# Delta rule: the next head's projection tiles dealt out in 11 portions of two to six per head instead of 18 of one to six

## What is computed

```
proj = rms_norm(x) @ w_in                       # q, k, v, z of each head
q, k, v = silu(conv(q)), silu(conv(k)), silu(conv(v))
q, k = l2_norm(q) * 128**-0.5, l2_norm(k)
m = strictly_lower(k_beta @ k.T * decay)
t_inv = inverse(eye + m)                        # triangular, unit diagonal
u, w  = t_inv @ v_beta, t_inv @ (k_beta * exp(g))
attn  = lower(q @ k.T * decay)
for each chunk:                                 # sequential
    v_new = u - w @ state
    o     = (q * exp(g)) @ state + attn @ v_new
    state = state * exp(g_last) + k_dec.T @ v_new
o = rms_norm(o) * silu(z)
```

## Time and profile before

| | before |
|---|---|
| median of 3 runs | 1638.53 us (1637.02 to 1641.39) |
| the profiled execution, its own time | 1640.73 us |
| its span in the profile | 1638.9 us |
| TensorE matmul busy | 1558.5 us, 95% of the span |
| VectorE busy | 624.2 us, 38% |
| ScalarE busy | 586.6 us, 36% |
| GpSimd busy | 577.8 us, 35% |
| mean granted TensorE clock | 0.986 of full speed |

### The profile page before, as it was taken

The page is one execution under the profiler, slowest core; times in us unless marked ns, Lnnn a source line. Parts: engine busy times, 40 slices in busy tenths (PEclk is TensorE's granted clock), DMA queues, the critical chain, the costliest instruction groups (busy, mean ns, idle before and its releaser), DMA issues.

```text
span 1638.9 us, 21277 instructions
## 1 busy us (share of the span) xinstructions
PE 1558.5 (95%) x7900; PEld 1277.1 (78%) x7900; DVE 624.2 (38%) x1014; ACT 586.6 (36%) x956; POOL 577.8 (35%) x286
## 2 busy tenths in 40 slices
PE   6899999999998989999999999887889999999998
PEld 6868878888787668888888887666668888888887
DVE  3336555665555432222122224677532222012210
ACT  6642243223332433322222234454533322222321
POOL 5531332223220234544434444211124443544442
PEclk9999999999999999999999999999999999999999
DMA  7411110111010123332333233111113332333222
GB/s 252 127 56 39 52 33 32 51 38 51 26 33 0 39 77 96 104 102 82 112 102 101 74 89 122 42 39 30 30 49 108 95 101 79 114 103 102 80 79 86
DMA packets 39208, 124.24 MB, mean 76 GB/s; under 512 B 4192, under 2 KB 5472, under 8 KB 39136
## 3 DMA queue, kind: packets, MB, share of 16 engines
q1 hardware_dynamic: 38976, 123.00, 25.0%
q10 hardware_dynamic: 160, 0.26, 0.1%
HBM read 120.89 MB, written 2.10 MB: 75 GB/s over the span
## 4 chain that ended last, share of the span: by engine, by line
PE 85%; DVE 6%; ACT 5%; issue 3%; DMA 0%; POOL 0%; SPq 0%; DVEq 0%; ACTq 0%
PE bank L548 66%; ACT ws L1044 4%; PE bank L713 3%; PE bank L711 2%; PE bank L699 2%; DVE ws L1426 1%; PE bank L977 1%; DVE ws L1432 1%; DVE act_lo L1432 1%; PE bank L847 1%; PE bank L810 1%; DVE ws L1435 1%; DVE ws L1429 1%; PE bank L736 1%; PE bank L1002 1%
## 5 line engine op out<-in xcount | busy, mean ns | idle before, releaser
L480 POOL TENSOR_TENSOR w_lo<-w_raw,w_hi 128x1024 fp32r<-128x1024 f32 (+1 forms) x250 | 537.8, 2168 | 949.8 <-ACT w_hi L1044 949.5
L548 PE MATMUL bank<-act_hi,w_hi 128*128 128x512 f32 (+1 forms) x1776 | 704.3, 397 | 10.0 <-POOL w_lo L480 4.4
L548 PE MATMUL bank<-act_hi,w_lo 128*128 128x512 f32 (+1 forms) x1776 | 681.0, 383 | 0.0
L548 PE MATMUL bank<-act_lo,w_hi 128*128 128x512 f32 (+1 forms) x1776 | 680.6, 383 | 0.0
L548 PEld LDWEIGHTS bank<-act_hi,w_hi 128*128 128x128 f32 x1776 | 336.2, 189 | 76.9 <-issue 7.8
L548 PEld LDWEIGHTS bank<-act_hi,w_lo 128*128 128x128 f32 x1776 | 335.6, 189 | 65.7
L548 PEld LDWEIGHTS bank<-act_lo,w_hi 128*128 128x128 f32 x1776 | 336.4, 189 | 63.8 <-issue 5.0
L1044 ACT ACTIVATE w_hi<-w_raw 128x1024 fp32r<-128x1024 f32 (+1 forms) x250 | 230.4, 953 | 89.1 <-PE bank L548 86.6
L1426 DVE TENSOR_TENSOR ws<-bank,ws 128x512 f32<-128x512 f32 x126 | 86.9, 690 | 371.5 <-PE bank L548 320.9
L1044 ACT ACTIVATE ws<-ws 128x512 f32<-128x512 f32 (+3 forms) x143 | 94.3, 670 | 189.2 <-DVE ws L1426 122.0
L1673 DVE TENSOR_TENSOR xT<-xT,bank 128x512 f32<-128x512 f32 (+1 forms) x48 | 33.0, 688 | 271.6 <-PE bank L548 271.6
(11 more groups left out here) (145 smaller groups left out, 1211.8 us busy)
## 6 DMA issues: line engine op xcount, KB each, us to landing
w_raw<-w_stream SPq DMA_DIRECT2D x154, 512.0 KB, 3.5
w_raw<-w_out SPq DMA_DIRECT2D x32, 384.0 KB, 3.2
w_raw<-w_down SPq DMA_DIRECT2D x32, 384.0 KB, 3.1
w_raw<-w_down SPq DMA_DIRECT2D x32, 320.0 KB, 3.2
ws<-x_in SPq DMA_DIRECT2D x1, 2048.0 KB, 8.4
ws<-mem_in SPq DMA_DIRECT2D x2, 512.0 KB, 4.0
out<-ws SPq DMA_DIRECT2D x1, 1024.0 KB, 4.2
sq_c<-squares_in SPq DMA_DIRECT2D x1, 768.0 KB, 6.3
```

The costliest lines, as they stand in the source:

```text
L480: nc.gpsimd.tensor_tensor(w_lo[:, s, 0:width * P], w_raw[:, s, 0:width * P], w_hi[:, s, 0:width * P].bitcast(F32), ALU.subtract).then_inc( ...
L548: mm = nc.tensor.matmul(acc, wt[:, c % RING, wsl], at[:, act0(k0 + k), off:off + n], start=(start and k == 0 and m == 0), stop=(stop and k ...
```

## The change

The same 32 tiles per head are issued, in the same order, by the same matmuls. The change moves where eleven of the portions stand in TensorE's list: projection 2 goes out as four portions of two tiles, each between P and TZ of levels 1 to 4, and no tile stands between TZ and the next P or in level 5. Projection 3 goes out as two tiles in each of the chunks 0 and 1 and four after the loop; nothing stands ahead of L723 or in chunks 2 and 3. The lists of the other engines are untouched.

```diff
-            LEVEL_FILL = (0, 2, 4, 6, 7, 8)
+            LEVEL_FILL = (0, 2, 4, 6, 8)
...
-                    if k <= 5:
-                        fill(2, range(LEVEL_FILL[k - 1], LEVEL_FILL[k - 1] + 1))
+                    if k <= 4:
+                        fill(2, range(LEVEL_FILL[k - 1], LEVEL_FILL[k]))
                     for g in range(2):
                         pe.wait_ge(S.p_done, n + g + 1)
...
                         mm.then_inc(S.tz_mm, 1)
-                    if k <= 3:
-                        fill(2, range(LEVEL_FILL[k - 1] + 1, LEVEL_FILL[k]))
-                fill(3, range(0, 1))
 
                 pe.wait_ge(S.tz_done, 12 * h + 12)
...
-                    fill(3, range(t + 1, t + 2))
+                    if t < 2:
+                        fill(3, range(2 * t, 2 * t + 2))
                     pe.wait_ge(S.v_done, n + 1)
...
                 mm.then_inc(S.o_done, 1)
-                fill(3, range(5, 8))
+                fill(3, range(4, 8))
```

## The result

The changed kernel takes 1662.8 us (median of 4 runs, 1661.4 to 1663.3) against 1640.0 us (median of 4, 1637.0 to 1642.3). The ratio is 1.0136, with a 95% interval of 1.0122 to 1.0149: 20 to 24 us slower. The forecast was 1658.5 with a range of 1654 to 1663. The span of the profiled execution grew from 1638.9 to 1661.5 us, by 22.6. One count ahead needs setting right: the change doesn't move eleven portions. Projections 2 and 3 went out in 14 portions per head and now go out in 7; with the four portions of projections 0 and 1, which stand as before, that makes the 18 and the 11 of the title.

A forecast was written before the change was run, and what follows sets the result against it. TensorE's matmul work, plus its holes, was taken to bound the kernel. Levels +1.80 and the part behind them +1.05 made +2.85 per head, +20.0 us over seven heads: 1658.5 us, range 1654 to 1663.

The forecast's parts named there:

- The levels: Levels 1 to 5 of each head: 21.40 us against 19.60 now, +1.80 for the same eight tiles.
- the price of an open passage: TZ to the next P with no tile between: 0.56 us, from level 5 at 3.98 against level 4 at 3.42.
- The cover over the tap: In levels with two tiles between P and TZ, these hide DVE's convolution tap and multiplications with 0.66 us to spare.
- The passage from P to TZ costs nothing uncovered: Inside a level, no added time without tiles, since DVE multiplies the first half while P works on the second.
- Behind level 6: From level 6's first step through the chunk loop to the sum on L753: +1.05 us per head.
- chunk 0 to 1: Chunk loop, one tile more: from 2.11 to 2.80 us, +0.69.
- The sum: Levels and the part behind them: +2.85 us per head, +20.0 us for seven heads; head 7 unchanged.
- Printed idle only: Rival: only the idle that the profile prints is lost, 0.9 us per head, 6 us in all, 1645; 4%.
- Tap in the path: Rival: the two tiles don't hide DVE's tap and multiplications in three levels, +14 us, 1672; 4%.
- Falling clock inside the heads: Rival: one slow stretch per head at 0.53 of the clock, +12 us on top, 1670; 2%.
- Boundaries: Rival: boundaries between portions cost more than waits, so faster, 1634 with every wait hidden; over 0.41 us each needed; 2%.
- The idle that I named before the first state product: Sign: no idle before L746 of chunk 0, new idles before L746 of chunk 2 and L748 of chunk 3.

The follow-up runs named there:

- r2: Only projection 2's portions moved (pairs between first and second step of levels 1 to 4), projection 3 as in the kernel before: 1655.0 us against 1638.4, ratio 1.0096.
- r4: Against the kernel before, projection 2 in pairs behind the second step of levels 1 to 4, projection 3 as before: ratio 1.0049, heads 7.3 to 7.7 us longer.
- r6: Against the kernel before, same tiles with six more portion boundaries per head where TensorE isn't waited for: ratio 1.0007, heads 1.0 to 1.3 us longer.

## Why the prediction was right

**The levels.** Forecast 4.11, three of 4.67, 3.28, sum 21.40; measured 4.10, then 4.66, 4.67 and 4.66, then 3.28, and 21.37 from 304.92 to 326.29. The step that mattered was to read the price of an open passage from the lengths of levels 4 and 5 and not from the idle column, which prints 0.18 for what costs 0.60 (r2 against the rival's 4 us). That the printed idle falls short of the cost is what these rows show; it doesn't follow from the ends being computed.

**The cover over the tap.** The forecast left 0.66 to spare. In the profile after, tap and multiplications end at 311.18 and L711 starts at 311.85, 0.67 later, with no idle. Right.

**From one step to the next inside a level.** "The passage from P to TZ costs nothing uncovered" held in bare levels (3.28, as in the earlier trace rows) and was my reason for giving level 5 no cost, which was right. As a general statement it is wrong: r4 shows 0.33 for it when the level's own start is covered. VectorE needs some 0.6 from the end of L699's first half to the end of its multiplication, in r4 as below; the second half of L699 lasts only 0.44. In a bare level that second half comes late anyway and the multiplication hides behind its wait (in level 5 after, the first multiplication runs from 323.77 to 324.19, while L699's second half starts only at 323.90), so only one of the two passages is paid.

```profile
302.62 0.87 DVE L1424 TENSOR_TENSOR ws<-bank,sq_c 128x256 f32<-128x256 f32 x2 [0.48 <-PE bank L699]
```

That is VectorE in r4's level 2, whose L699 starts at 301.98: the first multiplication can't start before 302.62, and the second step follows at 303.10 where TensorE was through with L699 at 302.87.

**Behind level 6.** From L699 of level 6 to L720 it takes 3.56, 3.57 before: the tile gave back 0.01, for a forecast of 0.02. Up to the first state product it takes 2.61 (forecast 2.59), in the bare chunks 1.81 and 1.91 (forecast 1.82 and 1.86), and behind the loop 3.07 (forecast 3.09). One term was mis-sized: chunk 0 to 1 took 2.69 and not 2.80. I had added a tile to 2.11, but the 2.11 held the starting lag of a wait that the change removes: L746 to L748 of chunk 0 took 0.33 before (318.67 to 319.00) and takes 0.22 after (L744 to L746, 332.46 to 332.68), so 0.1 had to come off. The part from L720 to L751 is 12.09 against 11.11 before, +0.98 for a forecast of +1.07.

**The sum.** Forecast +2.85 per head, 20.0 in all. Measured 19.4 to 19.9 over the seven heads in three profiles of each kernel.

**The time.** 1658.5 forecast, 1662.8 measured, 4.3 more. Of these, 1.4 are the kernel before itself, whose median with a fourth run is 1640.0 and not the 1638.5 that I added to. The other 2.9 stand over the forecast difference of 20.0. The heads gave nothing to them; 3.1 us came from the start of the kernel in this pair. The range had 1.5 us for scatter of any kind, so it held the result with nothing to spare, and that it did is partly luck. The mechanism and its size are what the prediction had right.

**The rivals.** Printed idle only: refuted by r2, 12.1 to 12.4 against 4. I had also priced it too low: the printed idle of the seven heads rose by 7.9 us (from 7.6 to 15.5) and not by 6. Tap in the path: no idle before L711. Falling clock inside the heads: 1.00 over the seven heads in every profile, and no projection tile in them shows the longer durations of a slow stretch. The Trainium skill ("TensorE: Matmul & The Clock Gate", A second HAM failure mode: psum-queue depth-cycling) tells of a kernel in which frequent short idles between groups of matmuls made the clock go up and down. The trace doesn't agree for this kernel: the seven heads, with nine idles of 0.16 to 0.51 us each, show none of it. Boundaries: 0.02 to 0.03 each in r6, where 0.41 was needed. The idle that I named before the first state product is gone, and those in chunks 2 and 3 are there, 0.16 each.

## What to carry to other kernels

When filler work is slipped into a chain between two engines, count portions by the gaps in which the other engine is late, and give each such gap one; a second tile in a gap that is covered already only takes cover from another. Price a gap by the distance between starts of two like stretches, one with and one without the cover; for TensorE neither the idle column nor the busy share shows it here (0.18 printed against 0.60, and a busy time that rose by 11.9 us in the heads for the same matmuls). When a gap turns out expensive, look next for open gaps in the old order: closing them gained 11 us here, half of what the change lost.

## What the runs showed of the hardware that I had not expected

A switch between an fp32 portion and an fp32r portion costs 0.02 to 0.03 us (r6), though the first matmul of a portion shows 0.48 where those behind it show 0.39 to 0.40. Most of what it loses the matmul ahead has gained: in r4 the last fp32 matmul of a second step stands 0.14 us ahead of the first tile (300.37 to 300.51), where two fp32 matmuls are 0.22 to 0.23 apart; the tile's first matmul then takes 0.31 to the next one instead of 0.23. And after one and the same idle of 2.37 us in the first stage, one execution kept a granted clock of 1.00 and another went on for 7.6 us at a mean of 0.80; kernels that differ only much later differ by up to 3 us there.
